# A Trainium2 kernel of two transformer blocks: the address of the moving tensor, the order of a short convolution's tiles, and the last row of a down projection

## The reference

```python
def short_conv_mixer(h, w_in, conv_w, conv_b, w_out):
    gate_b, gate_c, u = jnp.split(h @ w_in, 3, axis=-1)
    return (gate_b * dwconv3(gate_c * u, conv_w, conv_b)) @ w_out

def conv_ffn(h, w_up, conv_w, conv_b, w_down):
    a, val = jnp.split(h @ w_up, 2, axis=-1)
    return (jax.nn.gelu(dwconv3(a, conv_w, conv_b), approximate=False) * val) @ w_down
```

## Time and profile before

| | us |
|---|---|
| median of three runs | 2213.49 |
| the three runs | 2211.61 to 2214.72 |
| profiled execution | 2211.12 |
| its span | 2209.3 |
| TensorE busy | 2133.0 (97%) |
| VectorE busy | 1543.1 (70%) |
| ScalarE busy | 1127.5 (51%) |
| GpSimd busy | 274.4 (12%) |

### The profile page before, as it was taken

How to read it: one execution, slowest core, us unless ns; L and a number is a source line. 1 busy time by engine, 2 the same in 40 slices (tenths; PEclk the granted TensorE clock), 3 DMA queues, 4 the chain that set the end, 5 groups by cost and what they waited for, 6 DMA issues and landing times.

```text
span 2209.3 us, 40301 instructions
## 1 busy us (share of the span) xinstructions
PE 2133.0 (97%) x16826; PEld 2059.7 (93%) x16826; DVE 1543.1 (70%) x2684; ACT 1127.5 (51%) x1745; POOL 274.4 (12%) x256
## 2 busy tenths in 40 slices
PE   8999999999999999999999999999999999989998
PEld 7888899999998999999999999999879999989998
DVE  6777588764996777877777576573457886676664
ACT  5556578544444666554444454562245543435553
POOL 0000000001889445410000000000000000000000
PEclk9999999999999999999999999999899999999999
DMA  5433433566554444446777676322015767544563
GB/s 194 160 130 108 137 124 109 188 219 229 182 182 163 146 143 142 138 162 241 246 236 265 219 243 236 114 95 87 25 39 189 245 234 252 198 146 153 182 180 116
DMA packets 104005, 375.43 MB, mean 170 GB/s; under 512 B 11536, under 2 KB 12176, under 8 KB 103184
## 3 DMA queue, kind: packets, MB, share of 16 engines
q1 hardware_dynamic: 103824, 372.86, 50.2%
HBM read 370.71 MB, written 2.10 MB: 169 GB/s over the span
## 4 chain that ended last, share of the span: by engine, by line
PE 85%; DVE 7%; ACT 3%; POOL 2%; DMA 1%; issue 1%; SPq 0%; DVEq 0%; ACTq 0%
PE ps L365 24%; PE ps L366 23%; PE ps L367 23%; PE ps L696 3%; DVE wl L1428 2%; POOL wl L2117 2%; PE ps L449 1%; PE ps L495 1%; DMA raw<-in_ada 1%; PE ps L433 1%; PE ps L434 1%; PE ps L435 1%; PE ps L790 1%; PE ps L809 1%; ACT wh L997 1%
## 5 line engine op out<-in xcount | busy, mean ns | idle before, releaser
L365 PE MATMUL ps<-xah,wh 128*128 128x256 f32 x2944 | 850.9, 289 | 15.6 <-DVE xal L1453 5.2
L366 PE MATMUL ps<-xal,wh 128*128 128x256 f32 x2944 | 838.7, 285 | 0.0
L367 PE MATMUL ps<-xah,wl 128*128 128x256 f32 x2944 | 838.4, 285 | 0.0
L1428 DVE TENSOR_TENSOR wl<-raw,wh 128x1024 fp32r<-128x1024 f32 (+2 forms) x548 | 644.6, 1197 | 216.2 <-ACT wh L997 215.0
L997 ACT ACTIVATE wh<-raw 128x1024 fp32r<-128x1024 f32 (+1 forms) x608 | 620.1, 1036 | 300.2 <-PE ps L367 179.5
L365 PEld LDWEIGHTS ps<-xah,wh 128*128 128x128 f32 x2944 | 570.9, 194 | 27.7 <-issue 18.3
L366 PEld LDWEIGHTS ps<-xal,wh 128*128 128x128 f32 x2944 | 570.9, 194 | 0.5 <-issue 0.2
L367 PEld LDWEIGHTS ps<-xah,wl 128*128 128x128 f32 x2944 | 570.2, 194 | 0.0
L365 PE MATMUL ps<-hh,wh 128*128 128x256 f32 x1024 | 291.7, 285 | 9.5 <-DVE wl L1428 7.8
L366 PE MATMUL ps<-arenar,wh 128*128 128x256 f32 x1024 | 289.7, 283 | 0.0
L367 PE MATMUL ps<-hh,wl 128*128 128x256 f32 x1024 | 289.7, 283 | 0.0
(11 more groups left out here) (332 smaller groups left out, 2942.3 us busy)
## 6 DMA issues: line engine op xcount, KB each, us to landing
raw<-in_pu SPq DMA_DIRECT2D x128, 512.0 KB, 3.3
raw<-in_pv SPq DMA_DIRECT2D x128, 512.0 KB, 3.6
raw<-in_ada SPq DMA_DIRECT2D x96, 512.0 KB, 4.2
raw<-in_ff_up SPq DMA_DIRECT2D x88, 512.0 KB, 3.6
raw<-in_w_xbc SPq DMA_DIRECT2D x32, 512.0 KB, 3.3
raw<-in_ff_down SPq DMA_DIRECT2D x32, 512.0 KB, 3.7
raw<-in_w_z SPq DMA_DIRECT2D x16, 512.0 KB, 3.3
raw<-in_w_so SPq DMA_DIRECT2D x16, 512.0 KB, 4.1
```

The source lines that it names most:

```text
L365: mm(o, w0, x0, start=start, stop=False, skip_group_check=skip)
L366: mm(o, w0, x1, start=False, stop=False, skip_group_check=skip)
L367: return mm(o, w1, x0, start=False, stop=stop, skip_group_check=skip)
L1428: tt_(W.lo(i), W.raw(i), W.hi(i).bitcast(f32), ALU.subtract).then_inc(S["lowV"], 1)
```

## The change

Three edits.

1. `xah` and `xal` are laid out behind `pcol`, `cst`, `modc`, `mab` and `small`, not ahead of them. Nothing else changes its address.
2. The short convolution's tiles come in the order c0, u0, c1, u1, c2, u2, c3, u3, b0 to b3. VectorE makes the taps behind each u tile, tap by tap for its two rows in turn; the product with b comes behind each b tile and reads b from PSUM. `ogb` is gone.
3. The first down tile of each layer is `last_tile`: rows 0 to 20 of both halves, and row 21 of both at its end. In the first layer every down tile takes four modulation steps instead of three, and the short convolution takes three instead of seven.

```diff
-        xah, xal = sb(es, "xah", [128, 8, 256], f32r), sb(es, "xal", [128, 8, 256], f32r)
         pcol, cst = sb(es, "pcol", [128, NPC]), sb(es, "cst", [128, 2, 128])
         modc, mab, small = sb(es, "modc", [128, 2, 48, 2]), sb(es, "mab", [128, 5, 8]), sb(es, "small", [128, 64])
+        xah, xal = sb(es, "xah", [128, 8, 256], f32r), sb(es, "xal", [128, 8, 256], f32r)
...
-                        if half == 0:
+                        if half == 0 or (nk > 16 and k == 0):
                             next(between, None)
...
+            def last_tile(key, w, c, nk, x, need, between):
+
+                P, kept = take(key), []
+                for half in range(2):
+                    o = P[:, half * 256:half * 256 + 256]
+                    for k in range(0, nk, 8):
+                        n = min(8, nk - k)
+                        i, hi, lo = unit((key, half, k), w, c + half, k * 128, n * 128, 128)
+                        for q in range(n if k + n < nk else n - 1):
+                            need(k + q)
+                            last = product(o, hi[:, q, :], lo[:, q, :], x[0][:, k + q, :], x[1][:, k + q, :],
+                                           half == 0 and k + q == 0, False, skip=True)
+                        if k + n < nk:
+                            last.then_inc(W.used(i), 1)
+                        else:
+                            kept.append((i, o, hi[:, n - 1, :], lo[:, n - 1, :]))
+                        if half == 0 or k == 0:
+                            next(between, None)
+                need(nk - 1)
+                for half, (i, o, hi, lo) in enumerate(kept):
+                    last = product(o, hi, lo, x[0][:, nk - 1, :], x[1][:, nk - 1, :], False, True, skip=True)
+                    if half == 0:
+                        last.then_inc(W.used(i), 1)
+                last.then_inc(B.full(key, len(W.units)), 1)
+                W.done[i] = B.is_full(key)
...
-                for i in range(4):
+                last_tile(("down", l, 0), "ff_down", 8 * l, 22, XF, gated, late)
+                for i in range(1, 4):
                     tile(("down", l, i), "ff_down", 8 * l + 2 * i, 22, XF, gated, between=late)
...
-            for name in ("od_b", "od_c", "od_u"):
-                for i in range(4):
-                    if name == "od_b" and i == 0:
-                        first_tiles(((name, 0), name, 0), ((name, 1), name, 2), XA, od)
-                        next(late, None)
-                    elif name != "od_b" or i > 1:
-                        tile((name, i), name, 2 * i, 8, XA, od, between=late)
+            for i in range(4):
+                if i == 0:
+                    first_tiles((("od_c", 0), "od_c", 0), (("od_u", 0), "od_u", 0), XA, od)
+                else:
+                    tile(("od_c", i), "od_c", 2 * i, 8, XA, od, between=late)
+                    tile(("od_u", i), "od_u", 2 * i, 8, XA, od)
+            for i in range(4):
+                tile(("od_b", i), "od_b", 2 * i, 8, XA, od)
...
-                residual([("down", l, i) for i in range(4)], l, 40, range(0, 22, 8))
+                residual([("down", l, i) for i in range(4)], l, 40, ((0, 0), (0, 8), (0, 16), (1, 0)))
...
-                for k in (2 * i, 2 * i + 1):
-                    y = oyc[:, k, :]
-                    ts(y, cu[:, k, 1:257], pc("odw", 8 + k), pc("odb", k), ALU.mult, ALU.add).then_inc(own.up(), 1)
...
-                    tt_(y, y, ogb[:, k, :], ALU.mult).then_inc(S["oy"], 1)
+                at = [None, None]
+                for tap in (1, 0, 2):
+                    for a in range(2):
+                        k = 2 * i + a
+                        y, src = oyc[:, k, :], cu[:, k, tap:tap + 256]
...
+            run(late)
+            for i in range(4):
+                P = bank(("od_b", i))
+                v.wait_ge(own.sem, own.n)
+                for k in (2 * i, 2 * i + 1):
+                    tt_(oyc[:, k, :], P[:, 256 * (k % 2):256 * (k % 2) + 256], oyc[:, k, :], ALU.mult).then_inc(
+                        B.empty(("od_b", i)) if k % 2 else S["oy"], 1)
```

More of the change, by code:

```diff
@@ L283, in build @@
         cu = ar3[:, 20 * 256:20 * 256 + 8 * 258].rearrange("p (a b) -> p a b", b=258)
-        ogc, ogb, oyc = view(ar3, 29, 8, 256), view(ar3, 37, 8, 256), view(ar3, 45, 8, 256)
+        ogc, oyc = view(ar3, 29, 8, 256), view(ar3, 45, 8, 256)
         def v4(x):
@@ L1400, in act @@
                 shifted("od", k, hb, XA, md(1, 0, k))
[L1401 to L1404, removed]
             for i in range(4):
+                P = bank(("od_c", i))
+                put(flat(ogc[:, 2 * i:2 * i + 2, :]), P[:, :], ACT.Copy).then_inc(B.empty(("od_c", i)), 1)
                 halves(B.units[("od_u", i)] + AHEAD)
+            for i in range(4):
+                halves(B.units[("od_b", i)] + AHEAD)
                 for k in (2 * i, 2 * i + 1):
-                    a.wait_ge(S["oy"], k + 1)
+                    a.wait_ge(*(B.is_empty(("od_b", i)) if k % 2 else (S["oy"], i + 1)))
                     put(XF[0][:, k], oyc[:, k, :], ACT.Copy).then_inc(S["oy_h"], 1)
@@ L2033, in residual @@
                 for i in range(4):
-                    for k in beside:
-                        lows(W.at[keys[i], 0, k] + 1 + AHEAD)
+                    for half, k in beside:
+                        lows(W.at[keys[i], half, k] + 1 + AHEAD)
                         next(late, None)
@@ L2074, in dve @@
             v.wait_ge(own.sem, own.n)
[L2075 to L2081, removed]
             for i in range(4):
+                if i:
+                    lows(W.at[("od_c", i), 0, 0] + 1 + AHEAD)
+                    next(late, None)
+                lows(B.units[("od_c", i)] + AHEAD)
                 P = bank(("od_u", i))
@@ L2086, in dve @@
                 v.wait_ge(*B.is_empty(("od_u", i)))
-                for k in (2 * i, 2 * i + 1):
-                    y = oyc[:, k, :]
-                    ts(y, cu[:, k, 1:257], pc("odw", 8 + k), pc("odb", k), ALU.mult, ALU.add).then_inc(own.up(), 1)
[L2090 to L2093, removed]
-                    v.wait_ge(own.sem, own.n)
-                    tt_(y, y, ogb[:, k, :], ALU.mult).then_inc(S["oy"], 1)
+                at = [None, None]
[3 more added lines that the diff above has]
+                        y, src = oyc[:, k, :], cu[:, k, tap:tap + 256]
+                        if tap == 1:
+                            ts(y, src, pc("odw", 8 + k), pc("odb", k), ALU.mult, ALU.add).then_inc(own.up(), 1)
+                        else:
+                            v.wait_ge(*at[a])
+                            stt(y, src, pc("odw", 8 * tap + k), y, ALU.mult, ALU.add).then_inc(own.up(), 1)
+                        at[a] = (own.sem, own.n)
+            run(late)
+            for i in range(4):
+                P = bank(("od_b", i))
+                v.wait_ge(own.sem, own.n)
+                for k in (2 * i, 2 * i + 1):
+                    tt_(oyc[:, k, :], P[:, 256 * (k % 2):256 * (k % 2) + 256], oyc[:, k, :], ALU.mult).then_inc(
+                        B.empty(("od_b", i)) if k % 2 else S["oy"], 1)
                 for k in (2 * i, 2 * i + 1):
```

## The result

| | before | after |
|---|---|---|
| median, four runs each (us) | 2212.55 | 2196.11 |
| range (us) | 2211.11 to 2214.72 | 2192.47 to 2196.86 |
| profiled execution, its span (us) | 2211.12, 2209.3 | 2192.47, 2190.7 |

The ratio is 0.9928, with a 95% interval from 0.9916 to 0.9941: the change makes the kernel 0.7% faster. The forecast was 2198.0, in a range from 2190 to 2207.

What follows compares the result with a forecast made beforehand. TensorE, busy 97% of the span, was taken as the bound. Parts -12.0, -12.6, +3.4 and +5.7 sum to -15.5 us: 2195.6 from the profiled 2211.1, 2198.0 from the median 2213.5; range 2190 to 2207.

Steps and rivals of the forecast that it cites:

- Part A: Products with `xah`/`xal` moving: small buffers first ends their 64-byte alignment, 8832 matmuls gain 1.7 ns each; net -12.0 us.
- given back: Lines 433 to 435, `xah`/`xal` stationary: the aligned tensor is better there, so 192 matmuls lose 6 ns each, 1.2 us more.
- Part B: Short convolution: the new tile order leaves TensorE no wait and no half clock; -12.6 us.
- cover of 0.7 us: Short convolution, VectorE: a u tile's sums and next low take 5.0 us against 5.7 us of prepared matmuls.
- Rival 3: Short convolution: its sums are late for the lows, three places of 2 us each; 2204 us, chance 0.07.
- Part C: Down projections: `last_tile` gains 0, its held third unit brings new waits; +3.4 us second layer, +5.7 us first.
- 1.4 us: First layer, second down tile: wait for the second unit, whose load is issued late because the held unit keeps a `raw` slot.
- 0.9 together: First layer, second down tile: waits for the next two units, with the modulation's steps between; 0.9 us in all.
- fourth modulation step: First layer's down tiles: moves three loads from the short convolution; costs nothing by itself, VectorE having about 50 of 62 us work.
- Rival 1: Products with `xah` moving: its alignment gives nothing, as by the skill's cacheline rule; 2210 us, chance 0.13.
- rival 4: Products with `xah` moving: the offset costs instead of giving, 3 ns per product, 26.5 us; 2236.5 us, chance 0.03.
- rival 2: First layer's down stage: the held unit empties the slot ring, two more waits like the 4.2 us one; 2206 us, chance 0.10.

Runs made afterwards that it cites:

- B0: The kernel before the change, which the follow-up runs were measured beside; median 2212.55 us.
- A0: The changed kernel with all three edits; median 2196.11 us, ratio 0.9928 to the kernel before.
- the last experiment: Kernel without `last_tile`, 576 unused bytes ahead of `xah`, plus first-layer ScalarE and VectorE preparing two units further before the last up tile; 2164.8 us, ratio 0.9791.

## Why the prediction was right

**Part A, -12.0.** Right in size: 0.9946 is 11.9 us of 2210, with an interval from 9.1 to 14.6. The pitch after, 118.3 ns, is the others' (predicted 118), and 678 matmuls in 80 us is the number written down. The 512-column products with `xah` stationary went from 389 to 396 ns, as the term "given back" had it.

The *reason* was wrong, and it is luck that the number came out all the same: moved by 4576 bytes, `xah` changed its alignment and its distance from the weights at once, and came to the distance that the other tensors had. The prediction said: "`xah` starts at byte 61568 of a partition, a multiple of 64; every other moving tensor of these products starts 32 bytes past one". "Only the tensor that moves differs" was the step that failed: its distance from the weights differed too, a multiple of 512 bytes against 480 past one. The runs with shifted buffers show that neither address's place modulo 64 sets the pitch; the distance between the two operands does. Why it does is not shown. The reason held for the rows it was taken from because all tensors but one happened to share both properties. It failed in its first forecast on another layout, 2 to 3 us where 12.8 came.

Two smaller slips changed nothing. The "six tensors" in "five stages" are more than the earlier trace rows show, which are two pairs; the trace of B0 does have about 118.3 ns for all four pairs (`xbh`, `hh`, `xch`, `xfh` and their low parts). And 289 ns from start to end at a pitch of 119.9 are 2.4 matmuls at a time, not the "four matmuls" of the text.

**The rule weighed against it.** The Trainium skill's 16-byte cachelines ("SBUF — State Buffer", Specifications) would have given zero for every one of these shifts, all multiples of 16. The windows above have 669, 678 and 688 matmuls in the same 80 us, so the rule does not tell these layouts apart; it was right to go by the rows.

**Part B, -12.6.** Right: 0.9945, 12.2 us, interval 9.5 to 15.0, with the new modulation steps in it. The cover of 0.7 us on VectorE sufficed. The timeline of VectorE after, at the last gate tile, shows why the end needs no wait:

```profile
1956.22 0.75 DVE L2128 TENSOR_TENSOR arena<-ps,arena 128x256 f32<-128x256 f32 x2 [0.46 <-PE ps L367]
1957.13 0.76 DVE L2132 TENSOR_TENSOR xfl<-arena,xfh 128x256 fp32r<-128x256 f32 x2 [0.16 <-ACT xfh L1437]
```

Product to last subtraction is 1956.22 to 1957.89, 1.7 us, with 18 matmuls of rows 0 to 5 beside it; before, it was 5.4 us. The subtraction ends 1.7 us behind the end of TensorE's last b matmul (1956.19), where 2.2 was forecast, and 0.3 us before TensorE comes to row 6 (1958.15). Rival 3 did not happen: between the first layer's down stage and the last output tile, TensorE waits for no weights.

**Part C, +9.1.** Right in mechanism. The new wait is 2.4 us in both layers, forecast 2.3, and the run that releases the third unit earlier removes it. The gain of `last_tile` was put at zero, and it is: in neither layer was row 21 waited for, and the old 4.46 us wait is the same to 10 ns. What was mis-sized is the first layer's tail, "1.4 us" and "0.9 together": A0's trace has 0.2 us, at the fifth unit. The second unit's load was late, as forecast (ScalarE waited 2.93 us for it), and its low part was ready at 1831.03. At full clock TensorE would have come to it at about 1830.0 and waited 1.0 us; but 16 matmuls took 3.4 us rather than 1.9, and it came at 1831.62. I had added the half clock and the late loads as if they were apart. In the trace C comes to 2.4 + 1.5 + 0.2 in the first layer and 2.4 in the second, 6.5 us; the runs say 7.4 (A0 against the kernel without `last_tile`) and 8.8 (alone on B0), each known to 3 or 4 us. A0's profiled execution is the shortest of its four, 3.6 us below their median, so the others may well have had the second half-clock stretch; they have no profile here, and that stays open.

**The fourth modulation step, "costs nothing by itself".** Nearly. The kernel without `last_tile` has one wait of 1.07 us start to start at the fifth unit of the first layer's second down tile, where ScalarE waited for the load; the two kernels with 576 bytes and an ordinary tile have it too (1.14 and 1.08 us), and the kernel with the short convolution's part alone has the same four steps and no such wait.

**The sum, -15.5.** The two medians differ by 16.4. Measured, A was 0.1 and B 0.4 us short of the forecast, and C cost 1.7 us less, all well within what the intervals allow. The range's lower end was added up wrongly: A at -15, B at -12.6 and C at +3 give 2188.9, not 2190. None of rivals 1 to 5 came. Rival 1 was refuted by the windows, rival 4 by the sign, rival 2 by the last column of the small table of waits: no further gap of 4 us came.

## What to carry to other kernels

When one product's pitch differs between stages at the same clock with no wait, list the start addresses of *both* operands before blaming one: 32 unused bytes ahead of `xah` took some 3 ns off the pitch of its products here (669 against 688 in 80 us). Test such a cause with at least three layouts, since two tensors can't tell an address from a difference. Before a row is moved to a tile's end, ask which unit of weights it holds, and which work waits for that unit's slot: released one unit later instead of at the tile's end, it brought no new wait.

## What the runs showed of the hardware that I had not expected

- A float product of 128x128 by 128x256 takes some 116.7 to 120.0 ns on average from start to start at 2.4 GHz, depending on the distance in SBUF between the stationary and the moving tensor. Shifting both by 32 bytes leaves it unchanged (678 matmuls in 80 us, as in A0).
- At a distance of 32, the pitch can settle at 120 ns for 125 us behind a wait, or at 117.8 (669 and 681 against 688 matmuls in 80 us), with the distance unchanged.
- The 512-column products, whose moving tensor is the weights, go the other way: 389 ns from start to end with a distance that is a multiple of 512, 396 at 32 and 394 to 396 at 480. Row of line 433 (434 in the second, a line further down) in A0, then in the run with 32 bytes ahead of `xah`, where `xch` is at 512:

```profile
L433 PE MATMUL ps<-wh,xah x64: 392/396/802, 73.2 to 1501.6; 128*128 128x512 f32 x64
...
L433 PE MATMUL ps<-wh,xch x32: 393/394/398, 1441.7 to 1504.4; 128*128 128x512 f32 x32
```

```profile
L434 PE MATMUL ps<-wh,xah x64: 392/396/793, 72.4 to 1500.3; 128*128 128x512 f32 x64
...
L434 PE MATMUL ps<-wh,xch x32: 387/389/393, 1440.9 to 1503.1; 128*128 128x512 f32 x32
```

- Gaps of 2.5 us brought half clock for 13 to 16 matmuls in three places of four (A0 and `last_tile` alone on B0, two layers each), and none in the fourth. The 2.28 us gap of the last experiment brought it too, for about 15.
